# Differential attention in a four-layer decoder trunk: the last two heads with exchanged output banks, rotary steps together, and another order of quarters, turns and parts

## The chip, the cores and the metric

The kernel runs on one core of a Trainium2 chip. The metric is the device time of one launch in microseconds (us). Before the change three runs gave 2173.98, 2175.40 and 2177.06 us, median 2175.4.

## The reference

The input x is 512 tokens by 1024 features in float32. Four layers follow one another, each a token mixer and a dense feed-forward block, each of the two followed by a residual LayerNorm. Layers 0 and 3 have the mixer that the change touches, differential attention with 8 heads of 2 x 64:

```
qkv = x @ wqkv;  q, k get a partial rotary turn (16 of 64 lanes)
s = q . k / sqrt(64), causal, for each of the head's two maps
p = softmax(s);  a = p[0] - lam_full * p[1]
o = rms_norm(a @ v) * subln_g * (1 - lambda_init)
h = concat(o) @ wo
x = layer_norm(ALPHA * x + h)
```

Layer 1 has a convolution module, layer 2 a pooling mixer; their code is not touched.

## The kernel before

Everything is written out by hand: five engine programs (TensorE, VectorE, ScalarE, GpSimd and SyncE for loads) that run in their written order and meet only at semaphores. Nothing plans or reorders; the order of the calls in the source is the order on the engine. Float32 products are made exact enough by splitting both operands into a high and a low part: ScalarE copies the high part, VectorE subtracts it for the low part, and TensorE does three matmuls for each product (`exact`, lines 1489 to 1491).

Tokens are four blocks of 128 (TB = 4). A head j is worked in four query blocks c = 0..3, each with c + 1 key blocks. For one block the chain is:

- `scores(j, c)` on TensorE, two maps into PSUM banks 4 and 5 (c even) or 6 and 7 (c odd), with the causal mask added by a small bf16 matmul (lines 1783, 1786);
- `head_max(j, c)` on VectorE (line 1126), then `exps(j, c)` on ScalarE (line 815);
- `combine(j, c)` on VectorE: three tiny steps and the difference of the two maps (lines 1132 to 1137);
- `turn_diff(j, c)` on TensorE transposes the difference into bank 3 (line 1795), `turned(j, c)` on ScalarE copies it out (line 822), `values(j, c)` on TensorE multiplies it with v into the head's output bank (line 1806).

After the four blocks come `square` (ScalarE, line 827), `mean_square` (VectorE), a power on GpSimd (line 514), `norm_head` (VectorE, line 1146), `turn_head` (TensorE, four transposes back into the output bank, line 1813) and `out_head` (ScalarE, line 835), which writes the head's columns for the last projection.

The output bank is `o_bank(j)` (line 282): bank 2 for all heads but the last, bank 0 for the last. `values(j, 0)` waits until `out_head` of the head before has emptied the bank, except for the last head.

The q and k projections come from 16 units of weights, r = 0..15; unit r is 24 matmuls of 512 columns into bank r % 2, cut in four quarters (`unit(r, it, part)`) that are strewn between the attention steps. VectorE gives each unit its rotary turn: `rope_first` reads the bank (two instructions, then `rope_taken` counts up), `rope_second` makes the result (two more, then `roped`). `scores(j, 0)` waits for the units of its head. The last unit, 15, belongs to the last head.

The last projection (`wo`) has eight units of weights in a ring of four slots. `part(c, t)` is unit c for token block t: six matmuls into banks 2t and 2t + 1, three for each half. Parts of units 0 to 3 are strewn between the steps of the last head, and only into banks that are free by then: 4 to 7 are the score banks, 2 and 3 hold output and turned differences, 0 and 1 are the banks of the projection units. `chunk(c)` on ScalarE and VectorE splits a head's output for it, `split_w(w0 + c)` its weights. A part with `last` gives the slot free (`w_used`); units 4 to 7 follow in `down_end`, then the layer norm.

The stretch that the change touches is written out after the loop over heads: y is the head before the last (6), z the last (7). It is in lines 1196 to 1231 on VectorE, 1846 to 1912 on TensorE, and stands in both attention layers. ScalarE's order in it is not touched and is:

```
square(5), exps(y,0), exps(y,1), split_w(w0+1), turned(y,0), chunk(0), turned(y,1), chunk(1),
exps(y,2), chunk(2), exps(y,3), out_head(5), split_w(w0+2), turned(y,2), split_w(w0+3),
turned(y,3), chunk(3), exps(z,0), exps(z,1), square(y), turned(z,0), turned(z,1), exps(z,2),
exps(z,3), turned(z,2), out_head(y), turned(z,3), square(z), out_head(z)
```

Of the kernel before, what the change touches and what calls it, by code (L numbers as in the profile page):

```python
# [22 lines left out]
P = 128  # L23
# [162 lines left out]
def build(nc, x, wqkv, wo, lam, pw1, cln_g, cln_b, pw2, pw2_b, pool_w, pool_b, pool_s, w13, w2, g1, b1, g2, b2,  # L186
# [94 lines left out]

    def o_bank(j):

        return 0 if j == HEADS - 1 else 2


    raw_loaded = [sem(f"raw_loaded{r}") for r in range(RING)]
# [57 lines left out]
    def weight_hi(u):  # L345
        place = ahead_place(u)
        return f_hi[:, place[1], :] if place else w_hi[:, ring_number(u) % RING, :]
# [601 lines left out]
    def _(dve):  # L949
# [156 lines left out]
        for i in range(DEPTH):  # L1106
            mixer = MIXER[i % 3]
            if mixer == "attention":
# [40 lines left out]
                def rope_first(r, it=None):  # L1149

                    s, scale = r % 2, HD ** -0.5 if r % 2 == 0 else 1.0
                    dve.wait_ge(w_used, (0 if it is None else it * RING) + (u0 + r + 1))
                    nc.vector.scalar_tensor_tensor(mix_scratch[:, s, :], ps[:, s, :], scale, cst[:, C_COS:C_COS + SEQ],
                                                   ALU.mult, ALU.mult)
                    nc.vector.stream_shuffle(rope_scratch[:, s, :], ps[:, s, :], rope_lanes).then_inc(rope_taken, 1)

                def rope_second(r, it=None):

                    s, par, scale = r % 2, r // 2 % 2, HD ** -0.5 if r % 2 == 0 else 1.0
                    dve.wait_ge(rope_taken, at(it, 2, 2 * H0 + r + 1))  # L1160
                    link(nc.vector.scalar_tensor_tensor(qkT[:, par, s, :], rope_scratch[:, s, :], scale, cst[:, C_SIN:C_SIN + SEQ],
                                                        ALU.mult, ALU.mult), it, PER)
                    nc.vector.tensor_tensor(qkT[:, par, s, :], qkT[:, par, s, :], mix_scratch[:, s, :], ALU.add).then_inc(roped, 1)
# [35 lines left out]
                def chunk(c):  # L1199
                    split_a(hid[:, oT0 + c * SEQ:oT0 + (c + 1) * SEQ], c % RING, a0 + c + 1)  # L1200
# [9 lines left out]
                head_max(y, 3, None)  # L1210
                combine(y, 2, None)
                rope_first(2 * z + 1)
                combine(y, 3, None)
                rope_second(2 * z + 1)
                chunk(1)
                head_max(z, 0, None)
                head_max(z, 1, None)
                chunk(2)
                combine(z, 0, None)
                combine(z, 1, None)  # L1220
                mean_square(y, None)
                head_max(z, 2, None)
                split_w(w0 + 1)
                head_max(z, 3, None)
                combine(z, 2, None)
                split_w(w0 + 2)
                combine(z, 3, None)
# [258 lines left out]
    def _(pe):  # L1486
# [256 lines left out]
        for i in range(DEPTH):  # L1743
            mixer = MIXER[i % 3]
            if mixer == "attention":
# [51 lines left out]

                def values(j, c, it):
                    k = TB * (H0 + j) + c
                    if c == 0 and H0 + j and j < HEADS - 1:  # L1800
                        pe.wait_ge(oT_done, at(it, 1, H0 + j))
                    pe.wait_ge(diffT_done, at(it, TB, k + 1))
                    for kc in range(c + 1):
                        lo = kc * D + j * P
                        v = hid[:, lo:lo + P] if it is None else hid[:, bass.ds(it * (2 * P) + lo, P)]
                        e = nc.tensor.matmul(ps[:, o_bank(j), c * P:(c + 1) * P], diffT[:, c % 2, kc * P:(kc + 1) * P], v,  # L1806
                                             start=kc == 0, stop=kc == c)
                    e.then_inc(pv_done, 1)
# [40 lines left out]
                w0, a0, y = unit0[i, "wo"], chunks_before(i, "wo"), HEADS - 2  # L1849
                z = y + 1  # L1850

                def part(c, t, last=False):

                    chunk_ready(a0 + c + 1)
                    split_ready(w0 + c)
                    m = down_block((a_hi[:, c, :], a_lo[:, c, :]), w0 + c, t, c == 0, False)
                    if last:
                        m.then_inc(w_used, 1)

# [2 lines left out]
                unit(2 * z + 1, None, 0)  # L1862
                unit(2 * z + 1, None, 1)
                turn_diff(y, 0, None)
                scores(y, 2, None)
                turn_diff(y, 1, None)
                scores(y, 3, None)
                unit(2 * z + 1, None, 2)
                unit(2 * z + 1, None, 3)
                turn_head(y - 1, None)  # L1870
                values(y, 0, None)
                turn_diff(y, 2, None)
                values(y, 1, None)
                turn_diff(y, 3, None)
                values(y, 2, None)
                scores(z, 0, None)
                scores(z, 1, None)
                values(y, 3, None)
                turn_diff(z, 0, None)
                scores(z, 2, None)  # L1880
# [15 lines left out]
                part(2, 2)  # L1896
                values(z, 3, None)
                pe.wait_ge(oT_done, H0 + HEADS - 1)
                pe.wait_ge(diffT_done, TB * (H0 + HEADS))
                part(0, 1)  # L1900
                part(3, 2)
                part(1, 1)
                turn_head(z, None)
                part(2, 1)
                pe.wait_ge(oT_done, H0 + HEADS)
                part(0, 0, True)
                part(1, 0, True)
                part(2, 0, True)
                part(3, 0)
                part(3, 1)  # L1910
                part(3, 3, True)
                heads += HEADS
# [208 lines left out]
```

## Time and profile before

| what | value |
|---|---|
| median of three runs | 2175.4 us (2173.98 to 2177.06) |
| profiled execution | 2175.41 us, span of the trace 2173.6 us |
| TensorE (PE) busy | 2142.1 us, 99% |
| VectorE (DVE) busy | 1510.9 us, 70% |
| ScalarE (ACT) busy | 905.0 us, 42% |
| GpSimd (POOL) busy | 554.1 us, 25% |
| mean granted TensorE clock | 0.997 |
| a 512-column matmul of the projections (L1489, xT_hi) | 383 ns mean |
| load of one wo unit, issue to landing | 3.2 us median |
| the touched stretch, first attention layer | about 187 to 235 us of the span |
| the same, second attention layer | 1559.2 us later |

The span is the time from the first to the last instruction that the profiler saw; the rest of the 2175.41 us lies around it. Busy time counts compute instructions only. Matmuls are pipelined, so the start of one to the start of the next is the useful distance, not the duration in a row.

### The profile page before, as it was taken

What the parts mean: (1) busy time and instruction counts of PE and PEld (TensorE: products, weight loads), DVE (VectorE), ACT (ScalarE), POOL (GpSimd) and SP (SyncE); (2) the same over time, 40 slices, a digit from 0 to 9 for tenths busy, and PEclk for the clock granted to TensorE, in tenths of its full rate; (3) what the DMA queues carried; (4) which work ended last, traced back from release to release, by engine and by line L of the source; (5) the groups of instructions that cost most, each with busy time, mean ns of one, the idle gap of its engine ahead of it and who ended that gap; (6) DMA issues with size and microseconds to landing.
All of it is one profiled execution on the core that took longest, in us unless ns stands there. A gap on an engine that the chain in (4) does not pass through costs nothing.

```text
span 2173.6 us, 35563 instructions
## 1 busy us (share of the span) xinstructions
PE 2142.1 (99%) x13494; PEld 1899.8 (87%) x13494; DVE 1510.9 (70%) x2118; ACT 905.0 (42%) x1594; POOL 554.1 (25%) x386
## 2 busy tenths in 40 slices
PE   9999999999999999999999999999999999999998
PEld 7777899998888988999888899998887778999987
DVE  3688688873479978888634788853538868888534
ACT  2455445442333423445323444542335554445422
POOL 0000056630030002666300256610000001666100
PEclk9999999999999999999999999999999999999999
DMA  6211233433333022333521333342232113333421
GB/s 213 68 51 56 88 98 100 115 109 115 106 98 97 1 72 65 106 108 98 175 96 49 89 98 106 98 136 97 77 113 63 57 52 104 93 102 100 135 96 58
DMA packets 256749, 204.39 MB, mean 94 GB/s; under 512 B 6256, under 2 KB 235760, under 8 KB 256608
## 3 DMA queue, kind: packets, MB, share of 16 engines
q1 hardware_dynamic: 252976, 189.42, 29.3%
q0 software_dynamic: 3632, 13.02, 1.8%
q8 instruction: 97, 1.59, 0.3%
q14 instruction: 44, 0.36, 0.1%
HBM read 200.32 MB, written 2.10 MB: 93 GB/s over the span
## 4 chain that ended last, share of the span: by engine, by line
PE 91%; DVE 6%; issue 1%; ACT 1%; DMA 1%; SPq 0%; POOL 0%; DVEq 0%; POOLq 0%; ACTq 0%
PE ps L1489 17%; PE ps L1491 17%; PE ps L1490 17%; PE ps L1568 11%; PE ps L1570 11%; PE ps L1569 11%; DVE hid L1258 3%; PE ps L1783 2%; PE ps L1806 1%; PE ps L1614 1%; PE ps L1795 1%; PE ps L1786 1%; PE ps L1934 0%; PE ps L2029 0%; DVE x_nat L1021 0%
## 5 line engine op out<-in xcount | busy, mean ns | idle before, releaser
L962 DVE TENSOR_TENSOR w_lo<-raw,w_hi 128x1024 fp32r<-128x1024 f32 x196 | 248.1, 1273 | 337.0 <-ACT w_hi L585 336.6
L585 ACT ACTIVATE w_hi<-raw 128x1024 fp32r<-128x1024 f32 x196 | 203.7, 1055 | 381.0 <-PE ps L1491 367.6
L1489 PE MATMUL ps<-w_hi,a_hi 128*128 128x512 f32 x832 | 326.5, 392 | 3.6 <-DVE hid L1357 2.3
L1568 PE MATMUL ps<-t_hi,w_hi 128*128 128x256 f32 x1152 | 326.2, 283 | 3.2 <-DVE w_lo L1399 2.0
L1569 PE MATMUL ps<-t_lo,w_hi 128*128 128x256 f32 x1152 | 326.0, 283 | 0.0
L1570 PE MATMUL ps<-t_hi,w_lo 128*128 128x256 f32 x1152 | 326.0, 283 | 0.0
L1491 PE MATMUL ps<-w_hi,a_lo 128*128 128x512 f32 x832 | 324.6, 390 | 0.0
L1490 PE MATMUL ps<-w_lo,a_hi 128*128 128x512 f32 x832 | 324.5, 390 | 0.0
L652 ACT ACTIVATE w_hi<-raw 128x512 fp32r<-128x512 f32 (+1 forms) x288 | 212.4, 738 | 252.1 <-PE ps L1570 235.6
L1399 DVE TENSOR_TENSOR w_lo<-raw,w_hi 128x512 fp32r<-128x512 f32 (+1 forms) x288 | 268.9, 935 | 46.6 <-ACT w_hi L652 46.5
L1568 PE MATMUL ps<-xT_hi,w_hi 128*128 128x256 f32 x864 | 244.8, 283 | 0.0
L1569 PE MATMUL ps<-xT_lo,w_hi 128*128 128x256 f32 x864 | 244.5, 283 | 0.0
L1570 PE MATMUL ps<-xT_hi,w_lo 128*128 128x256 f32 x864 | 244.5, 283 | 0.0
L1489 PE MATMUL ps<-xT_hi,w_hi 128*128 128x512 f32 (+1 forms) x632 | 242.1, 383 | 1.4 <-issue 0.7
L1491 PE MATMUL ps<-xT_hi,w_lo 128*128 128x512 f32 (+1 forms) x632 | 235.0, 372 | 0.0
L1490 PE MATMUL ps<-xT_lo,w_hi 128*128 128x512 f32 (+1 forms) x632 | 234.3, 371 | 0.0
L1568 PEld LDWEIGHTS ps<-t_hi,w_hi 128*128 128x128 f32 x1152 | 221.1, 192 | 3.9 <-issue 3.7
L1569 PEld LDWEIGHTS ps<-t_lo,w_hi 128*128 128x128 f32 x1152 | 221.1, 192 | 0.2
L1570 PEld LDWEIGHTS ps<-t_hi,w_lo 128*128 128x128 f32 x1152 | 221.2, 192 | 0.0
L571 POOL TENSOR_TENSOR rstd<-var_eps,neg_half 128x1 f32<-128x1 f32 x32 | 17.7, 553 | 698.0 <-DVE var_eps L1016 693.6
L1489 PEld LDWEIGHTS ps<-w_hi,a_hi 128*128 128x128 f32 x832 | 156.6, 188 | 36.6 <-DVE hid L1357 2.7
L1491 PEld LDWEIGHTS ps<-w_hi,a_lo 128*128 128x128 f32 x832 | 156.6, 188 | 32.9
(170 smaller groups left out, 4227.1 us busy)
## 6 DMA issues: line engine op xcount, KB each, us to landing
raw<-in_w SPq DMA_DIRECT2D x264, 512.0 KB, 4.0
raw<-in_wqkv SPq DMA_DIRECT2D x48, 512.0 KB, 3.8
raw<-in_pw SPq DMA_DIRECT2D x24, 512.0 KB, 4.1
raw<-in_wo SPq DMA_DIRECT2D x16, 512.0 KB, 3.2
ln_gb<-in_g POOLq DMA_DIRECT2D x8, 512.0 KB, 4.4
ln_gb<-in_b POOLq DMA_DIRECT2D x8, 512.0 KB, 5.6
x_nat<-in_x SPq DMA_DIRECT2D x4, 512.0 KB, 5.6
out<-x_nat SPq DMA_DIRECT2D x3, 512.0 KB, 2.7
```

Source lines behind the costliest of these rows:

```text
L585: nc.scalar.activation(weight_hi(u), raw[:, r, :], ACT.Copy).then_inc(w_hi_done, 1)
L652: nc.scalar.activation(to, src, ACT.Copy).then_inc(form_hi[g], 1)
L962: nc.vector.tensor_tensor(weight_lo(u), raw[:, r, :], weight_hi(u).bitcast(f32), ALU.subtract).then_inc(w_lo_done, 1)
L1258: nc.vector.scalar_tensor_tensor(dws[c], src, cols[:, w:w + 1], dws[c], ALU.mult, ALU.add).then_inc(chain_step[stream], 1)
L1399: nc.vector.tensor_tensor(to, src, hi.bitcast(f32), ALU.subtract).then_inc(form_lo[g], 1)
L1489: nc.tensor.matmul(dst, lhs[0], rhs[0], start=start, stop=False, skip_group_check=check)
L1490: nc.tensor.matmul(dst, lhs[0], rhs[1], start=False, stop=False, skip_group_check=check)
L1491: return nc.tensor.matmul(dst, lhs[1], rhs[0], start=False, stop=stop, skip_group_check=check)
L1568: ms = [nc.tensor.matmul(dst, hi[:, at], x_hi, start=k == 0 and f in ("A11", "S1", "S2"), stop=False, skip_group_check=True), nc.tensor.ma ...
L1569: nc.tensor.matmul(dst, hi[:, at], x_lo, start=False, stop=False, skip_group_check=True),
L1570: nc.tensor.matmul(dst, lo[:, at], x_hi, start=False, stop=k == 3, skip_group_check=True)]
L1783: nc.tensor.matmul(ps[:, bank, 0:w], qkT[rows, j % 2, 0, c * P:w], qkT[rows, j % 2, 1, 0:w], start=True, stop=False)
```

## The change

The output banks of y and z are exchanged. The first block of y's values waits for the rotary step of unit 14 to have read bank 0, the first block of z's values for `out_head` of head 5. Quarters 2 and 3 of unit 15 move ahead of `scores(y, 2)` and ahead of `turn_diff(y, 1)` and `scores(y, 3)`. `turn_diff(y, 3)` moves behind `scores(z, 1)`. `part` can do one half; the half of part (0, 0) that goes to bank 1 is done ahead of `values(y, 3)`, the other half and the parts of token block 0 now come ahead of those of token block 1. On VectorE `rope_second` follows `rope_first`, and `chunk(1)` and `chunk(2)` come later.

```diff
@@ -281,7 +281,7 @@
 
     def o_bank(j):
 
-        return 0 if j == HEADS - 1 else 2
+        return 0 if j == HEADS - 2 else 2
 
 
     raw_loaded = [sem(f"raw_loaded{r}") for r in range(RING)]
@@ -1210,18 +1210,18 @@
                 head_max(y, 3, None)
                 combine(y, 2, None)
                 rope_first(2 * z + 1)
+                rope_second(2 * z + 1)
                 combine(y, 3, None)
-                rope_second(2 * z + 1)
-                chunk(1)
                 head_max(z, 0, None)
                 head_max(z, 1, None)
-                chunk(2)
                 combine(z, 0, None)
                 combine(z, 1, None)
+                chunk(1)
                 mean_square(y, None)
                 head_max(z, 2, None)
                 split_w(w0 + 1)
                 head_max(z, 3, None)
+                chunk(2)
                 combine(z, 2, None)
                 split_w(w0 + 2)
                 combine(z, 3, None)
@@ -1797,7 +1797,11 @@
 
                 def values(j, c, it):
                     k = TB * (H0 + j) + c
-                    if c == 0 and H0 + j and j < HEADS - 1:
+                    if c == 0 and j == HEADS - 2:
+                        pe.wait_ge(rope_taken, 2 * (H0 + HEADS) - 1)
+                    elif c == 0 and j == HEADS - 1:
+                        pe.wait_ge(oT_done, H0 + HEADS - 2)
+                    elif c == 0 and H0 + j:
                         pe.wait_ge(oT_done, at(it, 1, H0 + j))
                     pe.wait_ge(diffT_done, at(it, TB, k + 1))
                     for kc in range(c + 1):
@@ -1849,11 +1853,14 @@
                 w0, a0, y = unit0[i, "wo"], chunks_before(i, "wo"), HEADS - 2
                 z = y + 1
 
-                def part(c, t, last=False):
+                def part(c, t, last=False, halves=(0, 1)):
 
                     chunk_ready(a0 + c + 1)
                     split_ready(w0 + c)
-                    m = down_block((a_hi[:, c, :], a_lo[:, c, :]), w0 + c, t, c == 0, False)
+                    lhs = [a[:, c, t * P:(t + 1) * P] for a in (a_hi, a_lo)]
+                    for h in halves:
+                        m = exact(ps[:, 2 * t + h, :], lhs, [w[:, h * BANK:(h + 1) * BANK] for w in (weight_hi(w0 + c), weight_lo(w0 + c))],
+                                  c == 0, False)
                     if last:
                         m.then_inc(w_used, 1)
 
@@ -1862,19 +1869,21 @@
                 unit(2 * z + 1, None, 0)
                 unit(2 * z + 1, None, 1)
                 turn_diff(y, 0, None)
+                unit(2 * z + 1, None, 2)
                 scores(y, 2, None)
+                unit(2 * z + 1, None, 3)
                 turn_diff(y, 1, None)
                 scores(y, 3, None)
-                unit(2 * z + 1, None, 2)
-                unit(2 * z + 1, None, 3)
                 turn_head(y - 1, None)
                 values(y, 0, None)
                 turn_diff(y, 2, None)
                 values(y, 1, None)
-                turn_diff(y, 3, None)
                 values(y, 2, None)
                 scores(z, 0, None)
                 scores(z, 1, None)
+                turn_diff(y, 3, None)
+                pe.wait_ge(rope_taken, 2 * (H0 + HEADS))
+                part(0, 0, halves=(1,))
                 values(y, 3, None)
                 turn_diff(z, 0, None)
                 scores(z, 2, None)
@@ -1896,17 +1905,18 @@
                 part(2, 2)
                 values(z, 3, None)
                 pe.wait_ge(oT_done, H0 + HEADS - 1)
+                part(0, 0, halves=(0,))
+                part(3, 2)
+                part(1, 0)
+                part(2, 0, halves=(0,))
+                turn_head(z, None)
+                part(2, 0, halves=(1,))
+                part(3, 0)
                 pe.wait_ge(diffT_done, TB * (H0 + HEADS))
-                part(0, 1)
-                part(3, 2)
-                part(1, 1)
-                turn_head(z, None)
-                part(2, 1)
                 pe.wait_ge(oT_done, H0 + HEADS)
-                part(0, 0, True)
-                part(1, 0, True)
-                part(2, 0, True)
-                part(3, 0)
+                part(0, 1, True)
+                part(1, 1, True)
+                part(2, 1, True)
                 part(3, 1)
                 part(3, 3, True)
                 heads += HEADS
```

## Rows read from the trace of the kernel before

**Rows 1.** The page's busy times: engine, us, share of the span, instructions.

```profile
PE 2142.1 (99%) x13494; PEld 1899.8 (87%) x13494; DVE 1510.9 (70%) x2118; ACT 905.0 (42%) x1594; POOL 554.1 (25%) x386
```

**Rows 2.** Timeline of TensorE: start us, duration us, line, operation, [idle before <-releaser].

```profile
176.38 1.13 PE L1783 MATMUL ps<-hid 64*128 64x512 f32 x4
...
193.34 1.13 PE L1783 MATMUL ps<-hid 64*128 64x512 f32 x4
...
194.49 0.48 PE L1489 MATMUL ps<-xT_hi,w_hi 128*128 128x512 f32 x1
...
197.31 0.60 PE L1813 MATMUL ps<-cst,o_nat 128*128 128x128 f32 x4
...
198.69 0.49 PE L1806 MATMUL ps<-hid,diffT 128*128 128x128 f32 x2 [0.78 <-ACT hid L835]
...
200.18 0.63 PE L1795 MATMUL ps<-cst,diff 128*128 128x128 f32 x4 [0.23 <-ACT diffT L822]
...
200.64 0.83 PE L1806 MATMUL ps<-hid,diffT 128*128 128x128 f32 x6
...
202.80 1.11 PE L1806 MATMUL ps<-hid,diffT 128*128 128x128 f32 x8
...
205.13 0.33 PE L1795 MATMUL ps<-cst,diff 128*128 128x128 f32 x1 [1.22 <-DVE diff L1137]
...
208.84 0.50 PE L1489 MATMUL ps<-w_hi,a_hi 128*128 128x512 f32 x1
```

**Rows 3.** Timeline of TensorE, the same place in the second attention layer.

```profile
1757.93 0.49 PE L1806 MATMUL ps<-hid,diffT 128*128 128x128 f32 x2 [0.78 <-ACT hid L835]
```

**Rows 4.** Timeline of VectorE, heads 5 to 7.

```profile
177.76 1.23 DVE L1126 TENSOR_REDUCE neg_max<-ps 128x2 f32<-128x1024 f32 x1 [0.55 <-PE ps L1786]
...
190.72 0.35 DVE L1137 SCALAR_TENSOR_TENSOR diff<-prob,coef 128x128 f32<-128x128 f32 x1
...
194.72 1.23 DVE L1126 TENSOR_REDUCE neg_max<-ps 128x2 f32<-128x1024 f32 x1
...
196.38 0.62 DVE L1137 SCALAR_TENSOR_TENSOR diff<-prob,coef 128x384 f32<-128x384 f32 x1
...
203.61 0.68 DVE L966 TENSOR_TENSOR a_lo<-hid,a_hi 128x512 fp32r<-128x512 f32 x1
...
204.72 0.35 DVE L1137 SCALAR_TENSOR_TENSOR diff<-prob,coef 128x128 f32<-128x128 f32 x1
...
206.56 0.96 DVE L1126 TENSOR_REDUCE neg_max<-ps 128x2 f32<-128x768 f32 x1 [0.49 <-PE ps L1786]
```

**Rows 5.** Timeline of ScalarE, heads 5 to 7.

```profile
179.02 0.69 ACT L815 ACTIVATE prob<-ps,neg_max 128x512 f32<-128x512 f32 x1 [0.54 <-DVE neg_max L1126]
...
189.35 0.37 ACT L815 ACTIVATE prob<-ps,neg_max 128x128 f32<-128x128 f32 x1 [0.46 <-DVE neg_max L1126]
...
195.98 0.69 ACT L815 ACTIVATE prob<-ps,neg_max 128x512 f32<-128x512 f32 x1
...
197.95 0.69 ACT L835 ACTIVATE hid<-ps,gain 128x512 f32<-128x512 f32 x1 [0.52 <-PE ps L1813]
...
198.53 1.05 ACT L585 ACTIVATE w_hi<-raw 128x1024 fp32r<-128x1024 f32 x1
...
199.54 0.49 ACT L822 ACTIVATE diffT<-ps 128x384 f32<-128x384 f32 x1
...
201.35 0.63 ACT L588 ACTIVATE a_hi<-hid 128x512 fp32r<-128x512 f32 x1
```

**Rows 6.** The page's DMA issues: queue, count, size, us to landing.

```profile
raw<-in_wo SPq DMA_DIRECT2D x16, 512.0 KB, 3.2
```

**Rows 7.** Windows: busy us of each engine, granted TensorE clock (PEclk), DMA share, GB/s.

```profile
1062.00:1066.00 4.00, 1.73 (x9) 1.08 (x7) 4.00 (x3) 0.00 (x0) 4.00 (x2) 1.00 0.32 113
...
1066.00:1070.00 4.00, 4.00 (x11) 3.18 (x12) 4.00 (x2) 0.00 (x0) 4.00 (x2) 0.57 0.44 145
...
198.00:206.00 8.00, 5.87 (x44) 4.41 (x44) 7.12 (x22) 7.01 (x23) 0.00 (x0) 1.00 0.01 2
```

## The prediction

> **What bounds the kernel now.** I read the page's busy table first, then TensorE's waits, then the timelines of the stretch that the change touches, engine by engine. TensorE is busy for 2142.1 us of the 2173.6 us span [rows 1]; whatever keeps it standing or adds to its work moves the end, and what another engine does counts only through a wait of TensorE. So the question is how long TensorE stands in the last two heads (y = head 6, z = head 7), before and after.
>
> In the timeline of TensorE [rows 2] the reader sees three holds in brackets: 0.78 us before the first product with the values of y (it waits for out_head of head 5 on ScalarE), 0.23 us before turn_diff(y, 3) (it waits for turned(y, 2) on ScalarE), and 1.22 us before turn_diff(z, 0) (it waits for the difference of z on VectorE). That is 2.23 us in one attention layer. The second layer has the same stretch 1559.24 us later, with the same 0.78 [rows 3], so every figure below counts twice. From part(0, 2) at 208.84 on TensorE has work without a hold until the layer norm, and all that comes later hangs on it. Hence I measure one thing: how much later part(0, 2) starts, less the work that has been done ahead of it.
>
> **The bank exchange.** values(y, 0) now goes to bank 0, whose last reader was the rotary step of unit 14, long done, so the 0.78 us hold loses its cause. values(z, 0) waits for out_head(5) instead, which is over some ten microseconds before. By itself up to 0.78 us a layer won, if nothing else is late there.
>
> **The quarters ahead of scores.** Quarters 2 and 3 of unit 15 took 2.82 us after scores(y, 3) (194.49 to 197.31); now quarter 2 stands before scores(y, 2) and quarter 3 before scores(y, 3). The work is the same, except that each change from a small shape to the wide one makes the first matmul some 0.09 us longer (0.48 us in the row at 194.49 [rows 2]; the form has a mean of 0.38 in the page's table). Two such edges: scores(y, 3) moves from 193.34 to 193.34 + 2.82 + 0.18 = 196.34. This is the step that costs. Two chains hang on scores(y, 3), and the 2.8 us of matmuls that used to cover them now lie before it.
>
> VectorE first. Its order is max(y, 2), chunk(0), max(y, 3), combine(y, 2), so the difference of block 2 stands behind the maximum of block 3. From scores 3 to the start of its maximum 1.38 us (176.38 in [rows 2] to 177.76 in [rows 4], in head 5, where VectorE was waiting for it); from there to the difference of block 2 1.66 (194.72 to 196.38), 0.62 for itself, and 0.06 to TensorE (204.72 + 0.35 to 205.13): 3.72 us, so turn_diff(y, 2) can't start before 200.06. TensorE has until then scores(y, 3), 1.15 (193.34 to 194.49), turn_head 0.60 and values(y, 0) 0.32 or so: it is done at 198.4. A new hold of 1.7 us. Before the change the two quarters stood in this place, and the chain was covered.
>
> ScalarE second; its order is unchanged: exps(y, 3), out_head(5), split_w(w0 + 2), turned(y, 2). exps(y, 3) starts 1.26 us after the maximum (177.76 to 179.02 [rows 5]), at 196.34 + 1.38 + 1.26 = 198.98. It lasts 1.34 (195.98 to the end of work at 197.43, less the 0.11 by which one activation overlaps the next, as 197.95 + 0.69 against 198.53), out_head 0.58 (197.95 to 198.53), the weight split 1.01 (198.53 to 199.54), and turned(y, 2) to TensorE 0.64 (199.54 to 200.18). So values(y, 2) starts at 198.98 + 1.34 + 0.58 + 1.01 + 0.64 = 202.55. TensorE has only values(y, 1), under 0.6 us, after turn_diff(y, 2): a second new hold of about 1.7 us. The bank exchange gave back the right to start values(y, 0) early; out_head still stands on ScalarE ahead of the transposed block that TensorE needs next.
>
> **Turn and half part behind the scores of z.** values(y, 2), scores(z, 0) and scores(z, 1) take 2.16 us (200.64 to 202.80): turn_diff(y, 3) at 204.71. The rotary steps in one go are early enough: they start when combine(y, 2) is done, about 199.9, and four instructions of some 0.7 us end at 202.7, ahead of scores(z, 0). Then ScalarE, in its order: turned(y, 3), chunk(3), exps(z, 0). From turn_diff(y, 3) to chunk(3) 1.17 us (200.18 to 201.35, [rows 2, 5]), chunk(3) 0.52 (0.63 less the overlap), so exps(z, 0) at 206.40. Its maximum was ready at 204.6; the delay comes from the turn that was put behind the scores. From exps 0 to its difference 1.37 (189.35 to 190.72, [rows 4, 5]), then 0.35 + 0.06: turn_diff(z, 0) at 208.18, against 205.13. combine(z, 0) no longer waits behind chunk(2), but that matters only where VectorE is the late one, and here ScalarE is.
>
> In that interval TensorE does the half part, three matmuls. Twelve of this size took 2.82 us, so 0.70. Its added wait for the rotary reading of bank 1 (served at about 201.2) holds nothing, and chunk 0 is long split. values(y, 3), queued behind it, waits for turned(y, 3) anyway, so the half part is real work done in a hold: 0.70 us back, later on.
>
> **From there to part(0, 2).** Before: 205.13 to 208.84, 3.71 us. Now chunk(1), 0.68 us, stands before max(z, 2), where VectorE waited 0.49 (203.61 and 206.56 in [rows 4]): 0.19 more. chunk(2) before combine(z, 2) delays turn_diff(z, 2), which has part(0, 2) and part(1, 2), 2.8 us, as cover and uses nearly all of it; if that fails it costs some tenths. Sum for one layer: 3.05 + 0.19 - 0.70 = 2.54, which I round to 2.5 later.
>
> **The parts at the end.** Same matmuls, other order. The square, mean and norm chain of z keeps as many parts as cover, three in all; turn_head(z) now has one and a half parts behind it instead of one before out_head(z) is needed. The first ring slot of the wo weights is released one part (1.4 us) later relative to the end, four parts or 5.6 us before chunk 4 is needed; copying it on ScalarE (1.01) and the VectorE steps (about as long, plus 0.68) leave 2 us or more. part(3, 3), which releases the last slot, stays last. SP's load of w0 + 5 waits for VectorE's split of w0 + 1, now about 3 us later; a load takes 3.2 us [rows 6], and ScalarE wants it only after part(1, 1). I cost all this at nothing; if that cover were gone, it would be a few tenths.
>
> **The clock.** Of the 4.2 us from 198.4 to 202.55 TensorE works for under 1. With the present holds the granted clock stayed at 1.00 in 198 to 206 (5.87 us busy of 8). Elsewhere it did not: in 1062 to 1066 TensorE was busy 1.73 us of 4, and in the next 4 us 0.57 was granted, that is 1.2 instead of 2.4 GHz for 3.4 us, worth 1.7 us of work [rows 7]. So the ends are 0 and 1.7 a layer. The new stretch is emptier than the one that was punished, but a part of the slow time would fall into holds; I take 0.6 for both layers together. [...]
>
> **Sum.** 2 x 2.5 + 0.6 = 5.6 us. The profiled execution took 2175.41 us, span 2173.6, and equals the median of the three runs, 2175.4. Forecast: 2175.4 + 5.6 = 2181.0 us, a span near 2179.2.
>
> **Rivals.**
> First, faster: the new order does away with the holds. Without the 2.23 us, less 0.1 or 0.2 for edges, 2 x 2.2: 2171.0 us. Its place is turn_diff(y, 2); it decides if the difference is ready when TensorE is free, at 198.4. For it: the bank exchange really removes a cause, and the scores of z no longer stand behind turn_diff(y, 3). Against it: 3.72 us from four rows, with 2.1 us of work beside them. Chance 0.06.
> Second, a wash: the holds change place but not size, as when part of the chain runs earlier than I add up; 2175.4. Against it is the second hold, through ScalarE's fixed order. Chance 0.07.
> Third, the ScalarE link is shorter: turned(y, 2) gets in early and the hold shrinks by 1.1 us, after which the rotary steps (202.7) become what scores(z, 0) waits for, so that only about 0.5 us of it is won. 2.0 a layer, no clock loss: 2179.4. Chance 0.13.
> Fourth, the clock drops fully in both layers: 2175.4 + 5.0 + 3.4 = 2183.8. Chance 0.14.
> My forecast keeps 0.60; about 0.05 of it falls under the line.
>
> 0.2% is 4.35 us, about what runs of this kernel (2173.98 to 2177.06) can tell from no change. Slower: 0.55 + 0.14 = 0.69. Same: 0.05 + 0.07 + 0.13 = 0.25. Faster: 0.06. The range goes from 2177.6 (a layer's loss at 1.1 us) to 2184.0 (the fourth case); the wash and the faster case stay outside.
>
> **What will show it.** Right: no hold before values(y, 0), but one of about 1.7 us before turn_diff(y, 2) on the difference of VectorE, one of about 1.7 before values(y, 2) on diffT of ScalarE, and one of about 1 before turn_diff(z, 0); scores(y, 3) at 196.3, turn_diff(z, 0) near 208.2, part(0, 2) near 212.1; the same again 1562 us later. Wrong: turn_diff(y, 2) without a hold, max(y, 3) starting before 197, or a hold in the parts behind 212. The granted clock between 201 and 206, below 1.00 or not, settles the last term.

## The result, and the profile after

The changed kernel took 2181.71 us in the median of seven runs (2178.31 to 2183.74), the kernel before beside it 2173.98 (2171.62 to 2177.06): 7.7 us more, ratio 1.003 with a 95% interval of 1.002 to 1.004. The forecast was 2181.0. In a second session the same two kernels gave 2180.3 and 2175.14, 5.2 us apart.

The page's first lines for the changed kernel, to be read beside [rows 1]:

```profile
span 2176.7 us, 35572 instructions
...
PE 2141.0 (98%) x13493; PEld 1898.1 (87%) x13494; DVE 1509.9 (69%) x2118; ACT 904.7 (42%) x1594; POOL 552.3 (25%) x386
```

The span grew by 3.1 us and TensorE's busy time did not: what was added to the span is standing time. The span is that of one execution and the time varies by some us from one to the next, so I compare a stretch of the trace instead: from the start of scores(y, 0) to the start of part(0, 2). Before, in the first attention layer, it starts at

```profile
187.64 0.49 PE L1783 MATMUL ps<-hid 64*128 64x128 f32 x4
```

and ends at 208.84 [rows 2]: 21.20 us; in the second layer it takes 21.21. TensorE's timeline of the changed kernel (start us, duration us, line, operation, idle before and its releaser), first attention layer; the rows are scores(y, 0), scores(y, 3), values(y, 0), turn_diff(y, 2), values(y, 2), turn_diff(z, 0) and part(0, 2):

```profile
186.54 0.49 PE L1783 MATMUL ps<-hid 64*128 64x128 f32 x4
...
195.06 1.13 PE L1783 MATMUL ps<-hid 64*128 64x512 f32 x4
...
196.69 0.39 PE L1810 MATMUL ps<-hid,diffT 128*128 128x128 f32 x2
198.77 0.55 PE L1795 MATMUL ps<-cst,diff 128*128 128x128 f32 x3 [1.70 <-DVE diff L1137]
...
201.11 0.94 PE L1810 MATMUL ps<-hid,diffT 128*128 128x128 f32 x6 [1.34 <-ACT diffT L822]
...
206.79 0.33 PE L1795 MATMUL ps<-cst,diff 128*128 128x128 f32 x1 [0.97 <-DVE diff L1137]
...
210.65 0.50 PE L1489 MATMUL ps<-w_hi,a_hi 128*128 128x512 f32 x1
```

The reader is to see that values(y, 0) has no hold any more and three other places have one: 1.70 us, 1.34 us and 0.97 us, 4.01 in place of 2.23 [rows 2]. The stretch is 210.65 - 186.54 = 24.11 us, 2.91 more than before; 0.70 us of it is the half part done ahead, which leaves 2.21 us.

Behind part(0, 2) no hold of TensorE is named until the transposes of the normed x (line 1614) that wait for VectorE. They start, before and after, at

```profile
265.15 1.09 PE L1614 MATMUL ps<-cst,x_nat 128*128 128x128 f32 x8 [0.69 <-DVE x_nat L1021]
```

```profile
266.42 1.09 PE L1614 MATMUL ps<-cst,x_nat 128*128 128x128 f32 x8 [0.70 <-DVE x_nat L1021]
```

From part(0, 2) that is 56.31 us before and 55.77 after. So the half part gives back 0.54 us here and not 0.70, and from scores(y, 0) to these transposes the change costs 79.88 - 77.51 = 2.37 us. In the profiles of the versions below that have the half part, the loss at these transposes is 0.0 to 0.4 us a layer larger than the distance less 0.70 says; in the two that do not have it, the bank exchange and the quarters alone, the two measures agree within 0.02. Where the rest of the 0.70 goes I have not found out.

VectorE in the same stretch, the maximum of block 3 of y, the difference of block 2 and the maximum of block 0 of z (beside [rows 4]):

```profile
196.45 1.22 DVE L1126 TENSOR_REDUCE neg_max<-ps 128x2 f32<-128x1024 f32 x1 [1.38 <-PE ps L1786]
...
198.10 0.62 DVE L1137 SCALAR_TENSOR_TENSOR diff<-prob,coef 128x384 f32<-128x384 f32 x1
...
202.72 0.42 DVE L1126 TENSOR_REDUCE neg_max<-ps 128x2 f32<-128x256 f32 x1
```

ScalarE: out_head(5), split_w(w0 + 2), turned(y, 2), turned(y, 3), exps(z, 0) (beside [rows 5]):

```profile
199.05 0.68 ACT L835 ACTIVATE hid<-ps,gain 128x512 f32<-128x512 f32 x1
199.62 1.06 ACT L585 ACTIVATE w_hi<-raw 128x1024 fp32r<-128x1024 f32 x1
200.56 0.49 ACT L822 ACTIVATE diffT<-ps 128x384 f32<-128x384 f32 x1
...
204.01 0.60 ACT L822 ACTIVATE diffT<-ps 128x512 f32<-128x512 f32 x1 [2.01 <-PE ps L1795]
...
205.03 0.36 ACT L815 ACTIVATE prob<-ps,neg_max 128x128 f32<-128x128 f32 x1
```

Both chains are there as named. The difference, done at 198.10 + 0.62 = 198.72, releases turn_diff(y, 2) at 198.77. turned(y, 2), at 200.56, follows out_head and the split without a pause, 1.8 us after the transposes of its block began. exps(z, 0) starts at 205.03 behind turned(y, 3) and chunk(3), while its maximum was done at 202.72 + 0.42 = 203.14.

In the second attention layer the holds before turn_diff(y, 2) and values(y, 2) have the same sizes, but the matmuls behind them are slow. The rows are scores(y, 0), values(y, 2), scores(z, 0) and part(0, 2), and then come the windows (busy us of PE, PEld, DVE, ACT, POOL, granted clock, DMA share, GB/s):

```profile
1746.74 0.49 PE L1783 MATMUL ps<-hid 64*128 64x128 f32 x4
...
1761.31 1.05 PE L1810 MATMUL ps<-hid,diffT 128*128 128x128 f32 x6 [1.34 <-ACT diffT L822]
1762.29 0.80 PE L1783 MATMUL ps<-hid 64*128 64x128 f32 x4
...
1772.31 0.50 PE L1489 MATMUL ps<-w_hi,a_hi 128*128 128x512 f32 x1
```

```profile
1757.00:1761.00 4.00, 1.27 (x10) 0.88 (x8) 3.86 (x10) 4.00 (x10) 0.00 (x0) 1.00 0.00 0
1761.00:1765.00 4.00, 3.69 (x20) 2.41 (x21) 2.23 (x7) 1.20 (x2) 0.00 (x0) 0.62 0.00 0
```

scores(z, 0) takes 0.80 us here against 0.49 in the first layer, the clock granted in those four microseconds has a mean of 0.62 after four in which TensorE worked for 1.27, and the stretch is 25.57 us: 1.46 more. By the Trainium skill ("TensorE: Matmul & The Clock Gate", section "Why this matters for your kernels") idle gaps between bursts of matmuls send the clock back to half rate. The trace shows the fall, but behind two holds of 1.70 and 1.34 us with 1.00 us of matmuls between them, each shorter than the gap that the page names, and the same two holds in the first layer brought none; the measurement decides here.

At the transposes of line 1614 the two layers have lost 2.37 and 3.82 us, 6.2 together, and yet this span is only 3.1 us longer than that of the profile before. The rest goes with the clock in places that the change does not touch. In the profile before it fell in 12 to 16 us, to a mean of 0.63, and in 1066 to 1070, to 0.57 [rows 7], which by an estimate of 4 x 0.37 + 4 x 0.43 is worth up to 3.2 us; in the profile after it stayed at 1.00 in both places.

### The profile page after: what moved, and what is told of

It is laid out like the page before. It is cut to its first block, busy times and chain, and to the rows that moved or that the text cites. A ratio compares the mean times of both kernels' runs of the same rounds, so it can differ in the third digit from the quotient of the medians.

```text
span 2176.7 us, 35572 instructions
## 1 busy us (share of the span) xinstructions
PE 2141.0 (98%) x13493; PEld 1898.1 (87%) x13494; DVE 1509.9 (69%) x2118; ACT 904.7 (42%) x1594; POOL 552.3 (25%) x386
## 4 chain that ended last, share of the span: by engine, by line
PE 91%; DVE 6%; ACT 2%; issue 1%; DMA 1%; SPq 0%; POOL 0%; DVEq 0%; POOLq 0%; ACTq 0%
PE ps L1489 17%; PE ps L1491 16%; PE ps L1490 16%; PE ps L1568 11%; PE ps L1570 11%; PE ps L1569 11%; DVE hid L1258 3%; PE ps L1783 2%; PE ps L1810 1%; PE ps L1614 1%; PE ps L1795 1%; PE ps L1786 1%; PE ps L1944 0%; PE ps L2039 0%; DVE x_nat L1021 0%
```

## The experiments

Times are medians beside the kernel before on the same chip, ratios with their 95% interval. "Distance" is the stretch above, in the first attention layer where no other is named.

**The bank exchange alone.** The kernel before, with

```diff
-        return 0 if j == HEADS - 1 else 2
+        return 0 if j == HEADS - 2 else 2
...
-                    if c == 0 and H0 + j and j < HEADS - 1:
+                    if c == 0 and j == HEADS - 2:
+                        pe.wait_ge(rope_taken, 2 * (H0 + HEADS) - 1)
+                    elif c == 0 and j == HEADS - 1:
+                        pe.wait_ge(oT_done, H0 + HEADS - 2)
+                    elif c == 0 and H0 + j:
```

and the end parts of token blocks 0 and 1 swapped.

> The kernel before with the bank exchange alone: y's output in bank 0, z's in bank 2, the two new waits, and the end parts of token blocks 0 and 1 swapped to fit; quarters, turns, VectorE's order as before. Measure: from the start of scores(y, 0) to the start of part(0, 2), 21.20 us before (187.64 to 208.84). Theory (ScalarE's order out_head, split_w(w0+2), turned(y, 2) is what holds TensorE): the hold of 0.78 us before values(y, 0) goes, but turn_diff(y, 3) can't start before turned(y, 2), which still comes at the same time, so the 0.78 and the 0.23 become one hold of about 1.0 there; distance 21.2, time within 0.5 us of before. Rival (the hold was worth its length): distance 20.4, 1.6 us faster.

scores(y, 0), turn_diff(y, 3), part(0, 2):

```profile
186.01 0.49 PE L1783 MATMUL ps<-hid 64*128 64x128 f32 x4
...
198.48 0.63 PE L1795 MATMUL ps<-cst,diff 128*128 128x128 f32 x4 [1.20 <-DVE diff L1137]
...
207.21 0.50 PE L1489 MATMUL ps<-w_hi,a_hi 128*128 128x512 f32 x1
```

Distance 21.20, ratio 1.000 (0.9991 to 1.0009), 2175.14 against 2174.25. The two holds have become one of 1.20 before turn_diff(y, 3). The profile names VectorE as its releaser: its difference of block 3 ends at 198.39. ScalarE's turned(y, 2) ends at 198.33, so the two are tied, and ScalarE's order, which the expectation names as the cause, is only one of two. Within the interval the exchange is worth nothing alone.

**The two quarters alone.** The kernel before, with

```diff
                 turn_diff(y, 0, None)
+                unit(2 * z + 1, None, 2)
                 scores(y, 2, None)
+                unit(2 * z + 1, None, 3)
                 turn_diff(y, 1, None)
                 scores(y, 3, None)
-                unit(2 * z + 1, None, 2)
-                unit(2 * z + 1, None, 3)
```

> The kernel before with the two quarters of unit 15 moved alone (quarter 2 ahead of scores(y, 2), quarter 3 ahead of turn_diff(y, 1) and scores(y, 3)). Theory (two chains hang on scores(y, 3)): a hold of about 1.7 us before turn_diff(y, 2) on VectorE's difference (less 0.1 or so, as values(y, 0) still waits for out_head before it, in which case the hold is split or sits wholly before values(y, 0)), turned(y, 2) about 2 us later, distance from scores(y, 0) to part(0, 2) 23.5 us against 21.2: 2.3 us a layer, 4.6 us slower, and up to 1.5 us more a layer where the granted clock falls. Rival (the loss comes from turn_diff(y, 3) and the half part behind the scores of z, or from the end parts): distance 21.2, no slower.

scores(y, 0), values(y, 0), turn_diff(y, 3), values(y, 3), part(0, 2), and the windows:

```profile
185.99 0.49 PE L1783 MATMUL ps<-hid 64*128 64x128 f32 x4
...
199.23 0.49 PE L1806 MATMUL ps<-hid,diffT 128*128 128x128 f32 x2 [2.93 <-ACT hid L835]
...
200.72 0.88 PE L1795 MATMUL ps<-cst,diff 128*128 128x128 f32 x4 [0.23 <-DVE diff L1137]
...
204.85 1.11 PE L1806 MATMUL ps<-hid,diffT 128*128 128x128 f32 x8
...
210.89 0.50 PE L1489 MATMUL ps<-w_hi,a_hi 128*128 128x512 f32 x1
```

```profile
196.00:200.00 4.00, 1.07 (x10) 0.83 (x9) 3.86 (x12) 4.00 (x10) 0.00 (x0) 1.00 0.00 0
200.00:204.00 4.00, 3.77 (x23) 2.97 (x21) 2.50 (x5) 2.63 (x5) 0.00 (x0) 0.62 0.00 0
```

2181.77 against 2174.25, 7.5 us slower, ratio 1.0034 (1.0022 to 1.0046): this one edit does as much as the whole change. The hold is one, 2.93 us, before values(y, 0), because out_head is now behind the late exps(y, 3). Distance 24.90 (24.89 in the other layer). The clock fell to a mean of 0.62 after four microseconds with 1.07 of work. What that costs is read from the same matmuls: from turn_diff(y, 3) to values(y, 3) it is 204.85 - 200.72 = 4.13 us here and 202.80 - 200.18 = 2.62 before [rows 2], so 1.51. Without it the quarters alone cost 24.90 - 1.51 - 21.20 = 2.19 us a layer, which is the changed kernel's 2.21.

**The quarters put back** in the changed kernel, the same diff reversed.

> The changed kernel with only the two quarters put back behind scores(y, 3); bank exchange, turns, half part, VectorE's order and end parts as changed. Theory: scores(y, 3) comes early again and the quarters cover both chains; exps(z, 0) still waits behind turned(y, 3), so turn_diff(z, 0) is some 0.6 us later than before; distance about 22.0 us, of which 0.7 is the half part done ahead: time that of the kernel before within 1 us, 5 or more faster than the changed one. Rival (turns and half part cost it): distance 23 or more, still 3 us or more slower than before.

scores(y, 0), part(0, 2):

```profile
187.45 0.49 PE L1783 MATMUL ps<-hid 64*128 64x128 f32 x4
...
209.36 0.50 PE L1489 MATMUL ps<-w_hi,a_hi 128*128 128x512 f32 x1 [0.15 <-ACT prob L815]
```

Distance 21.91, less the half part 21.2. 2174.84 against 2174.25, ratio 1.0005 (0.9996 to 1.0014). The loss is that of the quarters. Everything else of the change costs 0.33 and 0.37 us in the two layers at the transposes of line 1614, and in time nothing that the interval can tell from zero.

**Fillers in the two new holds.** The changed kernel, with matmuls that no result uses:

```diff
+                def fill(exps, bank, n):
+                    pe.wait_ge(exp_done, exps)
+                    for _ in range(n):
+                        nc.tensor.matmul(ps[:, bank, 0:P], ident_b[:, :], mask_b[:, :], start=True, stop=True)
...
                 values(y, 0, None)
+                fill(TB * (H0 + y) + 3, S_BANK, 15)
                 turn_diff(y, 2, None)
                 values(y, 1, None)
+                fill(TB * (H0 + y) + 3, S_BANK, 11)
                 values(y, 2, None)
```

> The changed kernel with filler matmuls that no result uses (bf16, 128 columns, into a score bank that has been read): 15 ahead of turn_diff(y, 2) and 11 ahead of values(y, 2), so that TensorE works in the two new holds. If the fillers fit into the holds, nothing that is waited for moves. Theory (a part of the loss is the clock, which fell to 0.62 after these holds in the second attention layer of the changed kernel's profile, where the stretch took 25.57 us against 24.11 in the first): granted clock 1.00 in both stretches, 24.1 us in both, median some 1.5 to 3 us below the changed kernel's, 4 to 5 us above before, and less spread than 2178.3 to 2183.7. Rival (the clock's loss is rare or lies elsewhere): median as the changed kernel's, 7.7 us above before.

scores(y, 0), the first fillers, values(y, 2), part(0, 2):

```profile
185.99 0.49 PE L1783 MATMUL ps<-hid 64*128 64x128 f32 x4
...
196.70 1.01 PE L1870 MATMUL ps<-mask_b,ident_b 128*128 128x128 bf16 x15 [0.17 <-ACT prob L815]
...
200.56 0.94 PE L1810 MATMUL ps<-hid,diffT 128*128 128x128 f32 x6 [0.73 <-ACT diffT L822]
...
210.09 0.50 PE L1489 MATMUL ps<-w_hi,a_hi 128*128 128x512 f32 x1 [0.15 <-ACT prob L815]
```

The fillers took the room of the holds and moved nothing: distance 24.10 in both layers, granted clock 1.00. 2178.06 against 2174.25, 3.8 us slower, ratio 1.0019 (1.0010 to 1.0028). That is 2 x 2.2 = 4.4 within the error: the order without the clock of this stretch. At the transposes of line 1614 the order comes to 2.38 and 2.54 us, 4.9 for both layers.

**ScalarE: turned(y, 2) first.** The changed kernel, with

```diff
+                turned(y, 2, None)
                 out_head(y - 1, None)
                 split_w(w0 + 2)
-                turned(y, 2, None)
```

> The changed kernel; on ScalarE turned(y, 2) stands ahead of out_head(5) and split_w(w0+2) instead of behind them. Theory: the second new hold (1.34 us before values(y, 2) in the changed kernel) is ScalarE's order alone. turned(y, 2) comes 1.15 us earlier, but then scores(z, 0) waits for the rotary result, so the stretch from scores(y, 0) to part(0, 2) loses only about 0.5 us: 23.6 us against 24.11, 1 us for both layers, and up to 1 us more where the clock no longer falls. Rival (out_head or the split is what TensorE really waits for): distance unchanged.

scores(y, 0), scores(z, 0), part(0, 2):

```profile
186.30 0.49 PE L1783 MATMUL ps<-hid 64*128 64x128 f32 x4
...
201.24 0.49 PE L1783 MATMUL ps<-hid 64*128 64x128 f32 x4 [0.64 <-DVE hid L1163]
...
209.91 0.50 PE L1489 MATMUL ps<-w_hi,a_hi 128*128 128x512 f32 x1
```

Distance 23.61. The hold on ScalarE is gone; one of 0.64 on the rotary result (VectorE, line 1163) has come. The granted clock stayed at 1.00 in both layers. 2177.46 against 2174.45, ratio 1.0017 (1.0007 to 1.0026).

**ScalarE: exps(z, 0) first.** The changed kernel, with

```diff
-                turned(y, 3, None)
-                chunk(3)
                 exps(z, 0, None)
+                turned(y, 3, None)
                 exps(z, 1, None)
+                chunk(3)
```

> The changed kernel; on ScalarE exps(z, 0) stands ahead of turned(y, 3), and exps(z, 1) ahead of chunk(3). Theory: the third hold (0.97 us before turn_diff(z, 0)) comes from turn_diff(y, 3) behind the scores of z, which holds exps(z, 0) in ScalarE's queue although its maximum is ready. Now turn_diff(z, 0) comes right behind values(y, 3), and the distance is about 23.1 us, 2 us faster than the changed kernel for both layers. Rival: VectorE's combine is late by itself, distance 24.1.

scores(y, 0), scores(z, 0), turn_diff(z, 1), part(0, 2):

```profile
186.22 0.49 PE L1783 MATMUL ps<-hid 64*128 64x128 f32 x4
...
202.06 0.80 PE L1783 MATMUL ps<-hid 64*128 64x128 f32 x4
...
208.54 0.41 PE L1795 MATMUL ps<-cst,diff 128*128 128x128 f32 x2 [0.39 <-ACT diffT L822]
...
210.70 0.47 PE L1489 MATMUL ps<-w_hi,a_hi 128*128 128x512 f32 x1
```

The hold before turn_diff(z, 0) is gone and one of 0.39 stands before turn_diff(z, 1). Distance 24.48, not 23.1: the clock fell in both layers of this profile (scores(z, 0) 0.80 us again), and 24.48 - 1.4 is 23.1. 2178.94 against 2174.45, ratio 1.0022 (1.0013 to 1.0031). So the step is as expected only after the clock is taken off. The next run shows it without that: it adds this step to the one before, with the clock at 1.00 in both, and the distance goes from 23.61 to 22.67.

**Both changes of ScalarE's order**, the quarters left ahead.

> The changed kernel with both changes of ScalarE's order (turned(y, 2) ahead of out_head and split; exps(z, 0) ahead of turned(y, 3)), quarters left as changed. Theory: what is left is the VectorE chain behind scores(y, 3) (hold of 1.7 us before turn_diff(y, 2)) and the wait for the rotary result: distance 22.6 us, of which 0.7 is work done ahead, so still about 0.7 us a layer, 1.4 us, slower than before. Rival (ScalarE's order alone is the trouble, the quarters are harmless): faster than before, distance under 21.5.

scores(y, 0) and part(0, 2):

```profile
188.08 0.49 PE L1783 MATMUL ps<-hid 64*128 64x128 f32 x4
...
210.75 0.47 PE L1489 MATMUL ps<-w_hi,a_hi 128*128 128x512 f32 x1
```

Distance 22.67. 2176.82 against 2174.45, 2.4 slower, ratio 1.0011 (1.0002 to 1.0020); 1.4 was expected. With ScalarE's order mended the quarters still cost.

**A version that beats both.** From the changed kernel, quarters put back, ScalarE in the order of the diff, chunk(1) of VectorE between combine(y, 2) and rope_first:

```diff
 (TensorE)
                 values(y, 1, None)
+                pe.wait_ge(rope_taken, 2 * (H0 + HEADS))
+                part(0, 0, halves=(1,))
                 values(y, 2, None)
...
                 turn_diff(y, 3, None)
-                pe.wait_ge(rope_taken, 2 * (H0 + HEADS))
-                part(0, 0, halves=(1,))
                 values(y, 3, None)
 (ScalarE)
-                out_head(y - 1, None)
                 split_w(w0 + 2)
                 turned(y, 2, None)
+                out_head(y - 1, None)
                 split_w(w0 + 3)
-                turned(y, 3, None)
                 chunk(3)
                 exps(z, 0, None)
+                turned(y, 3, None)
                 exps(z, 1, None)
```

> A version meant to beat both. From the changed kernel: quarters 2 and 3 back behind scores(y, 3); the half part goes between values(y, 1) and values(y, 2); on ScalarE split_w(w0+2), turned(y, 2), out_head(5), split_w(w0+3), chunk(3), exps(z, 0), turned(y, 3), exps(z, 1); on VectorE chunk(1) goes between combine(y, 2) and rope_first. Theory: the quarters cover both chains, the half part covers the wait for the rotary result, and exps(z, 0) is no longer behind a turn. turn_diff(z, 0) comes about 1.2 us earlier than before and 0.7 us of work is done ahead of it: distance 20.0 us against 21.20, worth 1.9 us a layer, 3.8 us faster than before, 2170.5. Rival (the holds only move, as with the bank exchange): distance 21.2 or more, same time as before.

scores(y, 0), scores(z, 0), values(y, 3), turn_diff(z, 1), part(0, 2):

```profile
186.30 0.49 PE L1783 MATMUL ps<-hid 64*128 64x128 f32 x4
...
199.14 0.49 PE L1783 MATMUL ps<-hid 64*128 64x128 f32 x4
...
201.88 1.16 PE L1810 MATMUL ps<-hid,diffT 128*128 128x128 f32 x8 [0.73 <-ACT diffT L822]
...
204.53 0.41 PE L1795 MATMUL ps<-cst,diff 128*128 128x128 f32 x2 [0.32 <-ACT diffT L822]
...
206.69 0.48 PE L1489 MATMUL ps<-w_hi,a_hi 128*128 128x512 f32 x1
```

The half part stands where TensorE would have waited for the rotary result, and scores(z, 0) follows without a hold; what is left is 0.73 and 0.32. Distance 20.39 (20.38 in the other layer), 0.4 over the expectation. I took the 0.32 before turn_diff(z, 1), where square(y) stands ahead of turned(z, 0) on ScalarE, for most of it; the next version, which has that hold no more, is only 0.17 shorter. 2170.84 against 2174.45, 3.6 us faster, ratio 0.9986 (0.9977 to 0.9995). Measured a second time:

> The first faster version once more, unaltered. In its first measurement it was 3.6 us faster than before, and its successor with one more step, whose stretch is 0.2 us shorter still, only 1.9 us, both with wide intervals. Theory (twice 1.5 us, by distance 20.39 against 21.20 and 0.7 us of work done ahead): 3.0 us faster than before. Rival (the first gain was a lucky draw): 1 us or less.

2171.43 against 2174.88, 3.4 us faster, ratio 0.9984 (0.9975 to 0.9993), distance 20.39 in both layers.

**One step more**: turned(z, 0) ahead of square(y) on ScalarE, the maximum of (z, 2) ahead of mean_square(y) on VectorE.

> The faster version (quarters back, half part between values(y, 1) and values(y, 2), ScalarE's new order) with one more step: on ScalarE turned(z, 0) ahead of square(y), and on VectorE max(z, 2) ahead of mean_square(y). Theory: its hold of 0.32 us before turn_diff(z, 1) goes, distance 20.1 us against 20.39, 4.3 us faster than before in all. Rival (VectorE or exps(z, 2) becomes the late one): distance stays at 20.4, 3.6 us faster.

Distance 20.22, the hold before turn_diff(z, 1) gone, 0.1 over the expectation. But 2173.27 against 2175.14, ratio 0.9992 (0.9983 to 1.0001): 1.9 us faster and not clear of zero, where 4.3 was expected. Its interval overlaps the first version's. At the transposes of line 1614 it is 76.06 and 76.15 us from scores(y, 0), the first version 76.14 and 76.28 in one profile and 76.03 and 76.05 in the other: the 0.17 is not there any more. The mean granted clock of its eleven executions is 0.9975 against 0.9980 and 0.9981, which is about 1.2 us (an estimate, 0.00055 of 2175). So the step gains nothing, and most of the gap between the two versions is a slower clock; why it was slower stays open.

**The changed kernel and the fillers again**, side by side.

> The changed kernel once more, unaltered, beside the filler version on the same chip. Theory (the order costs 2.2 us a layer net, and the clock up to 1.5 us more in each): median 2 to 3 us above the filler version's and 6 to 7 above before; where a stretch of the profile shows a clock under 1.00 its distance is near 25.6 us, else 24.1. Rival (the first batch's gap between the two was chance between chips): median within 1 us of the filler version's.

> The filler version again, unaltered, beside the changed kernel. Theory: 4 to 4.5 us above before (twice 2.2 us of order, no clock), distance 24.1 in both layers. Rival: the same as the changed kernel.

The changed kernel: 2180.3 against 2175.14, 5.2 us, ratio 1.0030 (1.0019 to 1.0041). The fillers: 2178.98, 3.8 us again, ratio 1.0017 (1.0008 to 1.0026), distance 24.11 in both layers. The gap between them is 1.3 us here and was 3.9 between the two sessions before (7.7 and 3.8).

The rows are scores(y, 0), part(0, 0) and part(0, 2) of the changed kernel in its second profile:

```profile
185.88 0.49 PE L1783 MATMUL ps<-hid 64*128 64x128 f32 x4
...
203.70 0.78 PE L1489 MATMUL ps<-w_hi,a_hi 128*128 128x512 f32 x1
...
210.72 0.51 PE L1489 MATMUL ps<-w_hi,a_hi 128*128 128x512 f32 x1
```

Distance 24.84: here the slow clock came later, after scores(z, 0) and on the half part (0.78 us instead of 0.48), and part of it ran inside the last hold. In its other layer the clock stayed up and the distance was 24.09. So a drop costs from 0.7 to 1.5 us and does not come every time: two of four stretches in two profiles, one in each.

The mean granted clock, which each execution has on record, tells more than the few profiles can. Changed kernel 0.9969 (7 executions) and 0.9972 (8), the quarters alone 0.9968 (6), exps(z, 0) first 0.9965 (11): these are the versions whose profiles show a fall in this stretch. All the others, in none of whose profiles it fell here, lie from 0.9975 to 0.9983: fillers 0.9983 and 0.9980, kernel before 0.9978 or 0.9979 (in the later sessions; the first has none on record). Each single value is rounded to a thousandth. A thousandth of 2175 us is 2.2 us, so the changed kernel loses an estimated 1.3 to 2.0 us to the clock against the kernel before. Against the fillers it is 3.0 and 1.7.

Within one kernel the clock also falls elsewhere, and the spread of the times goes with it. Of the changed kernel's seven executions the two fastest have 0.998, the slowest 0.995. The first profile of the fillers (2176.79 us) has no fall at all; the second (2182.17 us) has none in this stretch but three elsewhere, near 12, 820 and 1070 us. The first of the three:

```profile
12.00:16.00 4.00, 4.00 (x15) 3.13 (x14) 1.64 (x2) 1.06 (x1) 1.79 (x3) 0.57 1.02 412
```

## Why the prediction was right

**The bank exchange** was put at "up to 0.78 us a layer won, if nothing else is late there", and the sum then let out_head's successors on ScalarE take it back. Right in the outcome: alone it moved the hold and saved nothing, though VectorE's difference of block 3 was as late as ScalarE.

**The quarters** were named as the step that costs. Right, and shown from both sides: alone 7.5 us slower, taken back 0.6 us from the kernel before, with 0 in its interval.

**The VectorE chain.** Forecast 3.72 us from scores(y, 3) to turn_diff(y, 2), measured 195.06 to 198.77 = 3.71; the hold 1.7 forecast, 1.70 measured.

**The ScalarE chain.** Forecast 6.21 us from scores(y, 3) to values(y, 2), measured 6.05: the hold is 1.34, where I wrote about 1.7. The split took 0.94 us to the next start where I had 1.01, turned(y, 2) 0.55 to values(y, 2) where I had 0.64 (TensorE started 0.06 us after the copy ended and not 0.15, as in the row that I used, where VectorE's difference ended at the same time), and I had not taken all of turn_diff(y, 2) and values(y, 1), 1.00 us together, off the hold.

**Turn and half part.** turn_diff(z, 0) forecast 3.05 us later, measured 206.79 - 186.54 against 205.13 - 187.64, 2.76. The half part stood in a hold as forecast, but 0.54 us came back for it in this profile where I had 0.70.

**The sum of a layer**: 2.54 forecast, 2.21 measured at part(0, 2). Two terms make the difference. The 0.18 that I charged for two more edges before scores(y, 3) did not show: it starts 8.52 us after scores(y, 0) and started 5.70 before [rows 2], 2.82 later, the length of the quarters and nothing more. The other is 0.16 in the ScalarE link. Farther on, at the transposes of line 1614, the loss is 2.37 us, and 4.9 and 5.1 for both layers in the two profiles of the fillers. So the order costs about the 5.0 of the forecast, but partly by luck: a chain 0.33 us too long against a half part that gives back less than I took off. The end parts, which I costed at nothing, have no hold; the bank exchange alone has token blocks 0 and 1 swapped at the end too and loses nothing there, which points to the split part for the missing tenths, but no run tests it alone.

**The clock** was the term that I sized by choice between 0 and 1.7 a layer, 0.6 for both. It was too small. Profiles show 1.46, 0.75 and twice 0 in four stretches of the changed kernel, 1.1 for both layers on average; the mean granted clock of its 15 executions gives 1.3 to 2.0 (the estimate above). With 4.9 for the order that makes 6.2 to 6.9 us, where I had 5.6. The measured medians differ by 7.7 and 5.2, the means of the same executions by 6.9 and 6.2. That the forecast of 2181.0 lies only 0.7 from the first median is luck as well: it started from 2175.4, and the kernel before beside it took 2173.98.

The rivals: the faster case and the wash are out by the interval. The third, a shorter ScalarE link, was built and behaves as written: the hold goes, the rotary result takes its place, 0.5 us a layer is won and the clock stays up. The fourth, a full drop in both layers, occurs in no profile of the changed kernel, but in both layers of the one with exps(z, 0) first, which has the same two holds.

## What to carry to other kernels

When a block of matmuls is moved ahead of an instruction, look at what hangs on that instruction in the other engines' queues: here 2.8 us of work was moved in front of the very step whose two chains (3.7 and 6.1 us) it had been covering. A buffer that comes free earlier gains nothing while the next waits behind it are as late; here two were, the copy on ScalarE and the difference on VectorE. Work done ahead in a hold is to be followed to a point far behind: of 0.70 us here some 0.5 came back. Cure the order on the waiting engines first, and put the loose work (the half part) where the next hold is.

## What was not expected of the hardware

Two holds of 1.70 and 1.34 us, with 1.00 us of small matmuls between, were followed by a fall of the granted clock from 2.4 to 1.2 GHz in four of six stretches: two of four in the changed kernel, two of two with exps(z, 0) first. Behind the single hold of 2.93 us it fell in both layers of its profile, behind holds of 1.70 and 0.64 us in none of four. With twenty-six bf16 matmuls of 128 columns in the holds it stayed at 1.00 in all four stretches, and every wait was left where it was. Four against four of six could still be chance; the mean granted clock of whole executions, 0.9983 and 0.9980 with the fillers and 0.9969 and 0.9972 without, speaks against it.
